# A three-block network on one core: the gated linear attention joined by scores instead of states, and the order of work at the stage changes and in the ssm loop

## The reference, cut to what matters

```python
HG_HEADS, HG_DK, HG_DV, HG_CHUNK = 8, 128, 128, 64

def first_block(x, ...):
    for i in range(DEPTH):                                  # DEPTH = 2
        x = x + 0.5 * swiglu(rms_norm(x, ffn1_norm[i]), ...)
        h = rms_norm(x, mix_norm[i])
        x = x + (moba_mixer(h, ...) if i % 2 == 0 else mamba2_mixer(h, ...))
        x = x + 0.5 * swiglu(rms_norm(x, ffn2_norm[i]), ...)

def hgrn2_chunkwise(q, fpre, v, lb):                        # in second_block
    q = jax.nn.silu(q)
    f = lbh + (1.0 - lbh) * jax.nn.sigmoid(fpre)
    k, logf = 1.0 - f, jnp.log(f)
    def step(S, inp):                                       # over the 4 chunks
        qc, kc, lfc, vc = inp
        b = jnp.cumsum(lfc, axis=2)
        inter = jnp.einsum('bhtd,bhde->bhte', qc * jnp.exp(b), S)
        decay = jnp.exp(jnp.where(mask, b[:, :, :, None, :] - b[:, :, None, :, :], -jnp.inf))
        A = jnp.einsum('bhtsd,bhsd->bhts', qc[:, :, :, None, :] * decay, kc)
        intra = jnp.einsum('bhts,bhse->bhte', A, vc)
        b_last = b[:, :, -1:, :]
        S_new = jnp.exp(b_last[:, :, 0, :])[..., None] * S + jnp.einsum(
            'bhsd,bhse->bhde', kc * jnp.exp(b_last - b), vc)
        return S_new, inter + intra
```

## Time and profile before

| | |
|---|---|
| median of 3 runs | 1348.39 us (1347.85 to 1348.75) |
| the profiled execution's own time | 1349.01 us |
| its span, first to last instruction | 1347.2 us |
| granted TensorE clock, mean | 0.998 of full speed |
| busy: PE, DVE, ACT, POOL | 1333.1, 957.4, 753.2, 218.9 us |
| busy share of PE | 99% |

### The profile page before, as it was taken

The page is one execution under the profiler, slowest core; times in us unless marked ns, Lnnn a source line. Parts: engine busy times, 40 slices in busy tenths (PEclk is TensorE's granted clock), DMA queues, the critical chain, the costliest instruction groups (busy, mean ns, idle before and its releaser), DMA issues.

```text
span 1347.2 us, 21455 instructions
## 1 busy us (share of the span) xinstructions
PE 1333.1 (99%) x8527; PEld 1157.2 (86%) x8527; DVE 957.4 (71%) x1026; ACT 753.2 (56%) x882; POOL 218.9 (16%) x199
## 2 busy tenths in 40 slices
PE   9999999999999999999999999999999999999997
PEld 7888888888888888888899988888888899888886
DVE  6666668857666676666677999667888766877586
ACT  6444455656444454444566678854444455657453
POOL 3500001101000020000000126220000001655740
PEclk9999999999999999999999999999999999999999
DMA  8665646526555555555544565488886554645341
GB/s 277 208 190 188 193 157 210 188 91 191 187 187 187 187 187 190 187 187 187 188 157 159 188 207 172 142 279 290 283 290 234 187 157 157 219 159 182 113 157 50
DMA packets 158292, 254.19 MB, mean 189 GB/s; under 512 B 8784, under 2 KB 99232, under 8 KB 156560
## 3 DMA queue, kind: packets, MB, share of 16 engines
q1 hardware_dynamic: 155136, 232.94, 53.4%
q0 software_dynamic: 2576, 18.45, 3.6%
q10 hardware_dynamic: 512, 1.85, 0.4%
HBM read 252.12 MB, written 1.08 MB: 188 GB/s over the span
## 4 chain that ended last, share of the span: by engine, by line
PE 97%; DVE 2%; ACT 1%; issue 0%; POOL 0%; POOLq 0%; DVEq 0%; ACTq 0%
PE psum L630 24%; PE psum L618 12%; PE psum L662 5%; PE psum L663 5%; PE psum L664 5%; PE psum L1910 4%; PE psum L1911 4%; PE psum L1912 4%; PE psum L450 3%; PE psum L451 3%; PE psum L452 3%; PE psum L429 3%; PE psum L431 3%; PE psum L430 3%; PE psum L1435 1%; PE psum L1436 1%
## 5 line engine op out<-in xcount | busy, mean ns | idle before, releaser
L391 DVE TENSOR_TENSOR w_lo<-raw,w_hi 128x2048 fp32r<-128x2048 f32 x220 | 512.7, 2332 | 204.8 <-ACT w_hi L383 204.5
L383 ACT ACTIVATE w_hi<-raw 128x2048 fp32r<-128x2048 f32 x220 | 420.6, 1912 | 174.6 <-PE psum L664 79.6
L630 PE MATMUL psum<-hT,w_hi 128*128 128x512 f32 x1408 | 335.8, 390 | 0.9 <-DVE hT L501 0.8
L630 PEld LDWEIGHTS psum<-hT,w_hi 128*128 128x128 f32 x1408 | 260.8, 188 | 54.2 <-issue 1.6
L618 PEld LDWEIGHTS psum<-hT,w_lo 128*128 128x128 f32 x1408 | 180.2, 191 | 6.5
L618 PE MATMUL psum<-hT,w_lo 128*128 128x256 f32 x1408 | 183.0, 283 | 0.0
L662 PE MATMUL psum<-w_hi,hidT_hi 128*128 128x512 f32 x320 | 125.0, 391 | 0.0
L663 PE MATMUL psum<-w_lo,hidT_hi 128*128 128x512 f32 x320 | 125.0, 391 | 0.0
L664 PE MATMUL psum<-w_hi,hidT_lo 128*128 128x512 f32 x320 | 124.5, 389 | 0.0
L507 POOL TENSOR_SCALAR meansq<-sumsq 128x2 f32<-128x2 f32 x7 | 6.0, 856 | 661.7 <-ACT xn L475 661.7
L712 ACT ACTIVATE hid<-psum 128x512 f32<-128x512 f32 x44 | 26.3, 598 | 150.7 <-PE psum L618 150.7
(11 more groups left out here) (381 smaller groups left out, 2049.9 us busy)
## 6 DMA issues: line engine op xcount, KB each, us to landing
raw<-in_ffn_w_up SPq DMA_DIRECT2D x88, 512.0 KB, 4.8
raw<-in_ffn_w_down SPq DMA_DIRECT2D x88, 512.0 KB, 4.2
raw<-in_ffn_w_gate SPq DMA_DIRECT2D x86, 512.0 KB, 4.7
raw<-in_w_in SPq DMA_DIRECT2D x72, 512.0 KB, 4.6
raw<-in_ssm_w_in SPq DMA_DIRECT2D x48, 512.0 KB, 4.6
raw<-in_attn_w_qkv SPq DMA_DIRECT2D x24, 512.0 KB, 4.7
ada_in<-in_w_ada POOLq DMA_DIRECT2D x8, 1536.0 KB, 8.2
raw<-in_ssm_w_out SPq DMA_DIRECT2D x16, 512.0 KB, 4.4
```

The source lines that it names most:

```text
L383: act.activation(w_hi[:, slot, :], raw[:, slot, :], ACT.Copy).then_inc(sem("hi_ready"), 1)
L391: dve.tensor_tensor(w_lo[:, slot, :], raw[:, slot, :], w_hi[:, slot, :].bitcast(F32), ALU.subtract)\
L630: pe.matmul(both, hi[:, k, at_:at_ + P], hT[:, k, :, :], start=k == 0, stop=False, skip_group_check=True)
```

## The change

Three things change.

- The gated linear attention carries no state. The chunks are joined by pairs: t = 0 is chunks 0 and 1, t = 1 is chunks 2 and 3. In tick 17 (`JOIN`) PE makes for each head and pair the scores of the first chunk's keys to the second chunk's queries, and then the scores of all keys of the first pair to all queries of the second; for the farthest of these DVE makes two more decayed operands (`hg_far`). ACT copies both from PSUM (`hg_next`, `hg_across`). In tick 18 (`OUT_A`) the output is these scores by the values. `hg_joint` holds `hg_att` and `hg_next` side by side. The transposes of keys, the three states and the two ticks 19 and 20 of this part go; the other attention stays at its ticks.
- The stage changes. `linear_unit` and `turned_chunk` do all products with the high part of the activations first, waiting for that alone, and those with the low part after; at the transposes, feature tiles 0 and 1 get a PSUM bank of their own (five banks in use), so that they are split one by one. `last_by_tokens` finishes the last output unit of the ssm one token half after the other, as the last block did already; attention's last two tiles are ordered so too. DVE adds the first half while PE works on the second.
- The ssm loop. ACT does `copy_z(0)` before the last two tiles of the convolution, and the squares of group pairs 0 and 1 at other places in the loop; POOL makes the first root one item later.

The core of the diff follows (`turned_chunk` changes as `linear_unit` does). For the ticks the added lines are shown; those that they replace are the ones of `K_ROWS`, `STATES_12`, `STATE_3` and `OUT_A` in the kernel above.

```diff
-        hg_att = zoned("att", "hg_att", [P, HEADS * TT, HG_C])
-        hg_k_rows = zoned("pair", "hg_k_rows", [P, HEADS * TT, P])
-        hg_s = [zoned("sum", "hg_s1", [P, HEADS, P]), zoned("sum", "hg_s2", [P, HEADS, P], offset=4096),
-                zoned("exp", "hg_s3", [P, HEADS, P])]
+        hg_joint = zoned("att", "hg_joint", [P, HEADS * TT, 2 * HG_C])
+        hg_att, hg_next = hg_joint[:, :, 0:HG_C], hg_joint[0:HG_C, :, HG_C:2 * HG_C]
+        hg_across = zoned("sum", "hg_across", [P, HEADS, P])
...
             for kk in range(4):
                 k = k0 + kk
                 if ready:
+                    pe.wait_ge(sem(ready[0] + "_hi"), ready[1] + k + 1)
+                for t in range(TT):
+                    a = a_hi[:, k, t * P:(t + 1) * P]
+                    pe.matmul(psum[:, banks[t], :], a, hi[:, kk, :], start=k == 0, stop=False)
+                    pe.matmul(psum[:, banks[t], :], a, lo[:, kk, :], start=False, stop=False)
+            for kk in range(4):
+                k = k0 + kk
+                if ready:
                     pe.wait_ge(sem(ready[0]), ready[1] + k + 1)
                 for t in range(TT):
-                    to = psum[:, banks[t], :]
+                    m = pe.matmul(psum[:, banks[t], :], a_lo[:, k, t * P:(t + 1) * P], hi[:, kk, :], start=False,
+                                  stop=k == tiles - 1)
+            m.then_inc(sem("unit_used"), 1)
+        def last_by_tokens(pe, unit, tiles, a_hi, a_lo, banks, first_done):
+            hi, lo = use_unit(pe, unit)
+            for t in range(TT):
+                to = psum[:, banks[t], :]
+                for kk in range(4):
+                    k = tiles - 4 + kk
                     a, b = a_hi[:, k, t * P:(t + 1) * P], a_lo[:, k, t * P:(t + 1) * P]
-                    pe.matmul(to, a, hi[:, kk, :], start=k == 0, stop=False)
+                    pe.matmul(to, a, hi[:, kk, :], start=False, stop=False)
                     pe.matmul(to, a, lo[:, kk, :], start=False, stop=False)
-                    m = pe.matmul(to, b, hi[:, kk, :], start=False, stop=k == tiles - 1)
-            m.then_inc(sem("unit_used"), 1)
+                    m = pe.matmul(to, b, hi[:, kk, :], start=False, stop=kk == 3)
+                m.then_inc(sem("unit_used" if t else first_done), 1)
...
-            return {2: (4, 5, 6, 7), 5: (2, 3, 4, 5), 6: (2, 4, 6, 7)}.get(n, (2, 3, 4, 6))[k // 2]
+            banks = {0: (2, 3, 4, 6, 7), 2: (4, 5, 6, 7, 2), 5: (2, 3, 4, 5, 6), 6: (2, 5, 4, 6, 7)}.get(n, (2, 3, 4, 6, 5))
+            return banks[k if k < 2 else k // 2 + 1]
 
         def turned_x(n, k):
-            return psum[:, turned_x_bank(n, k), (k % 2) * SEQ:(k % 2 + 1) * SEQ]
+            at_ = (k % 2) * SEQ if k >= 2 else 0
+            return psum[:, turned_x_bank(n, k), at_:at_ + SEQ]
+        def last_of_bank(k):
+            return k if k < 2 else k | 1
...
-                act.wait_ge(sem("xT"), KD * n + (k | 1) + 1)
+                act.wait_ge(sem("xT"), KD * n + last_of_bank(k) + 1)
...
+            for t in range(TT):
+                for k in (6, 7):
+                    wo_tile(3, k, (t,))
...
-            for h in range(2):
-                dve.wait_ge(sem("unit_used"), u + 3 + h)
-                add_half(dve, h, pair_banks(h))
+            dve.wait_ge(sem("unit_used"), u + 3)
+            add_half(dve, 0, pair_banks(0))
+            for t in range(TT):
+                if t:
+                    dve.wait_ge(sem("unit_used"), u + 4)
+                else:
+                    dve.wait_ge(sem("out_part"), 1)
+                add_half(dve, 1, pair_banks(1), (t,))
...
+            last_by_tokens(pe, FIRST_UNIT["ssm_out"] + len(OUT_UNITS) - 1, KI, yT_hi, yT_lo, OUT_BANKS[1], "out_part")
...
                         split_hi(act, FIRST_UNIT["ssm_z"] + SLOTS)
+                        copy_z(0)
...
-            copy_z(0)
             for j in range(1, ITEMS // 2):
                 if j in (3, 5, 7):
                     copy_z(j // 2)
-                if j == 7:
-                    group_squares(1)
                 exps(2 * j)
                 exps(2 * j + 1)
+                if j == 5:
+                    group_squares(0)
                 if j < 7:
                     cross_exps(j + 1)
                 if j == 6:
...
                 if j == 3:
                     silu_z(0)
                     silu_z(1)
-                if j == 4:
-                    group_squares(0)
                 if j == 5:
                     group_scale(0)
+                if j == 6:
+                    group_squares(1)
...
+                if i == 10:
+                    group_rstd(0)
                 if i in (7, 10):
                     q = (i - 7) // 3
                     cs = slice(512 * q, 512 * (q + 1))
                     pool.wait_ge(sem("y"), 4 * (q + 1))
                     pool.wait_ge(sem("z_silu"), q + 1)
                     pool.tensor_tensor(y[:, :, cs], y[:, :, cs], z[:, :, cs], ALU.mult).then_inc(sem("y_gated_early"), 1)
-                if i in (9, 13):
-                    group_rstd((i - 9) // 4)
+                if i == 13:
+                    group_rstd(1)
...
-        K_ROWS, STATES_12, STATE_3, OUT_A, RET_TURN, RET_SCORES, RET_STATE, OUT_B = range(STEPS + 3, STEPS + 11)
+        JOIN, OUT_A = STEPS + 3, STEPS + 4
+        RET_TURN, RET_SCORES, RET_STATE, OUT_B = range(STEPS + 7, STEPS + 11)
...
+            if i == JOIN:
                 pe.wait_ge(sem("hg_decayed"), 2)
                 pe.wait_ge(sem("hg_att"), STEPS)
+                chunk = lambda c: slice(c * HG_C, (c + 1) * HG_C)
                 for n in range(HEADS * TT):
                     h, t = divmod(n, TT)
+                    m = pe.matmul(psum[0:HG_C, 4 + n // 8, n % 8 * HG_C:(n % 8 + 1) * HG_C],
+                                  hg_k[:, h, chunk(2 * t)], hg_q[:, h, chunk(2 * t + 1)], start=True, stop=True)
+                m.then_inc(sem("hg_joined"), 1)
+                pe.wait_ge(sem("hg_far"), 2)
                 for h in range(HEADS):
+                    for c, q in ((2, hg_q), (3, hg_pair)):
+                        for rows, k in ((0, hg_pair), (1, hg_k)):
+                            at_ = h % 4 * P + (c - 2) * HG_C
+                            m = pe.matmul(psum[chunk(rows), 6 + h // 4, at_:at_ + HG_C],
+                                          k[:, h, chunk(rows)], q[:, h, chunk(c)], start=True, stop=True)
+                m.then_inc(sem("hg_joined"), 1)
             if i == OUT_A:
+                pe.wait_ge(sem("hg_taken"), 2)
+                def both_chunks(h, t):
+                    pe.matmul(psum[:, 4 + 2 * t + h // 4, h % 4 * P:(h % 4 + 1) * P],
+                              hg_joint[0:HG_C, h * TT + t, :], hg_v[0:HG_C, t, h * P:(h + 1) * P],
+                              start=h % 4 == 0, stop=False, skip_group_check=True)
+                def second_chunk(h, t):
+                    return pe.matmul(psum[HG_C:P, 4 + 2 * t + h // 4, h % 4 * P:(h % 4 + 1) * P],
+                                     hg_att[HG_C:P, h * TT + t, :], hg_v[HG_C:P, t, h * P:(h + 1) * P],
+                                     start=False, stop=t == 0, skip_group_check=True)
+                for t in range(TT):
+                    for n, h in enumerate((0, 4, 1, 5, 2, 6, 3, 7)):
+                        both_chunks(h, t)
+                        if n:
+                            second_chunk((0, 4, 1, 5, 2, 6, 3, 7)[n - 1], t)
+                    m = second_chunk(7, t)
+                    for h in range(HEADS if t else 0):
+                        m = pe.matmul(psum[:, 6 + h // 4, h % 4 * P:(h % 4 + 1) * P], hg_across[:, h, :],
+                                      hg_v[:, 0, h * P:(h + 1) * P], start=False, stop=True, skip_group_check=True)
+                    m.then_inc(sem("out_a_ready"), 1)
...
+            if i == JOIN + 1:
+                act.wait_ge(sem("hg_joined"), 1)
+                act.activation(hg_next[:, :, :], psum[0:HG_C, 4:6, :].rearrange("p b (n t) -> p (b n) t", t=HG_C), ACT.Copy)\
+                   .then_inc(sem("hg_taken"), 1)
+                act.wait_ge(sem("hg_joined"), 2)
+                act.activation(hg_across[:, :, :], psum[:, 6:8, :].rearrange("p b (h t) -> p (b h) t", t=P), ACT.Copy)\
+                   .then_inc(sem("hg_taken"), 1)
...
+                dve.wait_ge(sem("hg_decayed"), 2)
+                dve.wait_ge(sem("hg_ends"), 2)
+                dve.wait_ge(sem("hg_products"), STEPS)
+                for own, c, over in ((hg_k, 0, 1), (hg_q, 3, 2)):
+                    cs = slice(c * HG_C, (c + 1) * HG_C)
+                    dve.tensor_tensor(hg_pair[:, :, cs], own[:, :, cs],
+                                      hg_last[:, :, over:over + 1].broadcast_to([P, HEADS, HG_C]), ALU.mult)\
+                       .then_inc(sem("hg_far"), 1)
```

(48 more changed lines are left out.)

67 lines of the change are left out of this document (8 added, 59 removed).

## The result

The changed kernel takes 1356.34 us (median of 6 runs, 1354.2 to 1358.37) where the kernel before takes 1348.30 on the same chip (1347.49 to 1349.22). The ratio is 1.0057, 95% interval 1.0045 to 1.0069.

The account below looks back on a forecast made before the run. PE bounds the kernel, busy 99% of the span and 97% of the chain. Gated attention 3.3, stage changes 3.3, start 0.3 and ssm loop 0.4 make 7.3 us, from 1348.39 to 1341.1; range 1339.0 to 1345.6.

Parts of the forecast that it names:

- Outputs: Gated attention's output piece, tick 18: 16 pairs of differently shaped products run side by side, 3.8 us.
- the first rival: Output piece: the two differently shaped products run one after the other, 7.9 us instead of 3.8; 1345.2 us, chance 0.14.
- every change of shape drains the array: Output piece, tick 18: 0.20 us for each of 31 shape changes, on top of no overlap; 1351.4 us, chance 0.07.
- return to units: Gated attention: first unit matmul behind a float32 piece takes 0.43 instead of 0.23; two such, 0.4 us.
- the lower bound of 9.9: Gated attention after the change: lowest time in us, a gain of 3.6; the sum taken was 10.2.
- scores: Gated attention: products inside pairs 2.1 us and across pairs 2.1 us, the wait for `hg_far` between them hidden.
- Stage changes: Six changes, n = 1 to 6: gaps between transposes and first matmul shrink, 3.3 of 3.7 us gained.
- the third rival: Stage-change gaps return a few matmuls on and POOL's root stalls the ssm loop: 1345.1 us; chance 0.15, wholly or half.
- Start: First FFN unit: the ACT and DVE chain PE waits for starts 0.2 to 0.4 earlier, 0.3 us gained.
- Ssm loop: Standstills of 1.04 and 0.76 us mostly become waits for DVE and ACT; 0.4 us gained together.
- its lower bound: Ssm loop: -1.0 us, as POOL's root stands ahead of an input PE wants and takes about a microsecond.
- The change doesn't do what it says: Whole kernel: PE only took up slack, so a shorter list moves the end less; no separate chance given.

Follow-up runs that it names:

- the kernel with halves of one shape: Changed kernel with all 32 output products on 64 rows and 128 columns, row halves in turn in different banks, their sum left out: 1341.14 us, ratio 0.9947.
- the groups of eight: Changed kernel with the 32 output products reordered, eight of one tile shape then eight of the other, 3 shape changes instead of 31: 1345.09 us, ratio 0.9973.
- groups of two: Changed kernel with the 32 output products reordered, two of each tile shape in turn, 15 shape changes: 1352.86 us, ratio 1.0035.

## Why the prediction was wrong

The step that failed is "Outputs, 16 pairs of one product on 64 rows and all columns with one on the other 64 rows and 64 columns. Side by side a pair costs 0.228 [...] to 0.248". Forecast 3.8 us, with the products across 5.6; measured 22.5 with what the units behind lost. The 16.9 us between split into three:

- No overlap: 32 products at 0.22 are 7.0, not 3.8: 3.2. This was the first rival, and its reason (different shapes) is shown by the kernel with halves of one shape.
- Changes of shape: 28 groups (14 of each shape), at 0.20 and 0.14, and 0.2 at the products across: 4.9. This was the rival "every change of shape drains the array"; its price of 0.20 was right for one shape and too high for the other (0.14), and its count of 31 was a little high, since at the ends of each 128 tokens two of a shape meet.
- The clock: 8.8, the remainder, in the profiled execution, which was the slowest of the six. No rival had it. Without it the kernel would have been level with the one before, as 26.7 - 8.8 = 17.9 against 13.5, less the 3.9 gained elsewhere, says: +0.5. So the forecast gain was lost to the two terms of shape, and the loss that is clear of noise is the clock's. The rival that said "slower" (1351.4 us) had the place and the mechanism, but got its sign by prices that were too high: 10.3 us over the forecast for overlap and changes together, where 8.1 were measured.

Two judgments led there. The drains got 0.07 because "the two output pieces before differ in shape and meet without a gap", and the rule that said otherwise was outweighed by that one seam. But the pieces of a chain meet without a gap where a change costs 0.2 us too, as the groups of eight show. Nor was it the only change of shape in the trace of before, as the prediction has it. Every piece on a part of the array begins and ends with one, and behind the earlier trace rows the chain goes on:

```profile
1297.77 1.09 PE psum L2045 x16
1298.86 0.43 PE psum L1910
```

These are 8 products on 64 rows and all columns, the row halves in turn, behind the 16 on the whole array of L2040. Four times 0.22 are 0.88, so 0.2 is left for the change. The 1.98 for 8 state products and the 1.99 for 16 are eight times 0.22 and the same 0.2, which the prediction spread over the products as 0.248 and 0.124. And it booked the first unit matmul's 0.43 instead of 0.23 as a "return to units", though that stands for the very thing: behind products of the whole array it takes 0.23. And 0.124 for halves of one shape was carried over to a pair of two shapes because only the rows were thought to matter. (A slip without weight: the lower bound of 9.9 adds up to 10.0.)

The other steps, by the trace: scores 3.88 us for 4.2, no wait between the two kinds, returns 0.4 for 0.4. Stage changes: 3.1 for 3.3, all six between 1.69 and 1.85 us, and the gaps did not come back later (start, stage changes and ssm loop make 4.0, and 3.86 of it was there at 1078.73), so the third rival falls. The runs put the same parts at 3.3. Start: 0.68 for 0.3, by the start of the transposes at n = 1 (193.49 for 194.17). Ssm loop: 0.2 for 0.4, nothing in the runs. What was late next is DVE's `cross` at the first standstill, as forecast; at the second it is POOL's inputs behind the root and the gating, which the prediction had only as its lower bound, while it counted on ACT's scaling. "The change doesn't do what it says" falls too: what PE's list gained or lost, the end gained or lost.

## What to carry to other kernels

- Sort small products by tile shape, or pad them to one shape. A quarter of zeros in a block cost nothing here; with 16 full products instead of 32 alternating ones the output piece took 5.4 us instead of 21.7.
- Price an alternation from a row that alternates. A seam in the chain shows no price, since its pieces meet without a gap also where a change costs 0.2 us. Compare the piece's time with its number of products instead. And where a rule speaks against one row and the pattern repeats some 30 times, it deserves more than one chance in fourteen.
- When a piece of PE work is thinned out, look at the granted clock by windows, not at busy time: here 8.8 of the 16.9 us over the forecast were the clock's.

## What the runs showed of the hardware that was not expected

- A group of products of another tile shape costs 0.20 us (64 rows, all columns) or 0.14 (64 rows, 64 columns) at its start, whatever its length from one to eight, also across different banks. Products on the whole array pay about 0.2 behind products on 64 rows.
- Products on different row halves of one shape overlap fully: 0.118 us each for 32 in a row, against 0.22 one after the other. The halves went to different banks there; whether they overlap in one bank no run asks.
- The clock fell to 0.50 while PE read as fully busy, 3 to 6 us into a stretch of shape changes. It came back 2.4 to 5.6 us after the last change of shape within the alternation, in groups of two still in the products across, in the changed kernel 2 us into the units. When it falls and comes back differs from kernel to kernel, and the runs of one kernel spread by up to 4 us.
